# Banded attention by key blocks 0..127, 128..255, 256..271 instead of meta keys and window blocks

## The reference, cut to what matters

```python
k = k.reshape(b, L, A_KV_HEADS, A_HEAD_DIM)              # L = 272
s_loc = einsum(q_block, k_of_this_and_the_block_before) + bias   # masked outside the window of 128
s_meta = einsum(q_block, k[:, :16]) + bias
p = softmax(concat([s_meta, s_loc, sink]))
o = p[..., :16] @ v_meta + p[..., 16:272] @ v_local
x = LayerNorm(ALPHA * x + (o * silu(gate)) @ w_out)
```

## Time and profile before

| | |
|---|---|
| median of 3 runs | 956.26 us (954.53 to 956.31) |
| the profiled execution | 955.46 us |
| its span, first to last instruction | 953.2 us |
| TensorE busy | 918.1 us |
| VectorE busy | 553.1 us |
| ScalarE busy | 427.4 us |
| GpSimd busy | 65.1 us |
| mean granted clock of TensorE | 0.990 of full |
| bytes moved | 153.04 MB, mean 161 GB/s |

### The profile page before, as it was taken

How to read it: one execution, slowest core, us unless ns; L and a number is a source line. 1 busy time by engine, 2 the same in 40 slices (tenths; PEclk the granted TensorE clock), 3 DMA queues, 4 the chain that set the end, 5 groups by cost and what they waited for, 6 DMA issues and landing times.

```text
span 953.2 us, 18688 instructions
## 1 busy us (share of the span) xinstructions
PE 918.1 (96%) x7496; PEld 893.3 (94%) x7496; DVE 553.1 (58%) x713; ACT 427.4 (45%) x667; POOL 65.1 (7%) x86
## 2 busy tenths in 40 slices
PE   4999999999999999978999999999999999999995
PEld 4999999999899999978999999999999999999995
DVE  4457675676556666696645545453645546455556
ACT  5446556455455433344534344444444444443330
POOL 1220230233020000003000000000000000000000
PEclk9999999999999999989999999999999999999998
DMA  8745553554362354522544434534344444444522
GB/s 279 240 155 192 176 161 134 168 168 127 132 210 96 126 179 174 187 79 98 212 169 144 169 138 171 179 133 176 132 176 151 157 154 154 176 171 184 193 115 89
DMA packets 24530, 153.04 MB, mean 161 GB/s; under 512 B 3328, under 2 KB 3344, under 8 KB 7728
## 3 DMA queue, kind: packets, MB, share of 16 engines
q1 hardware_dynamic: 20736, 140.52, 40.5%
q0 software_dynamic: 2896, 7.70, 4.2%
q10 hardware_dynamic: 864, 4.33, 1.2%
HBM read 150.35 MB, written 2.18 MB: 160 GB/s over the span
## 4 chain that ended last, share of the span: by engine, by line
PE 88%; DVE 5%; DMA 3%; ACT 1%; issue 1%; SPq 0%; DVEq 0%; ACTq 0%
PE bank L246 73%; DMA raw<-chunks 3%; PE bank L334 2%; PE bank L521 2%; DVE w_lo L807 2%; PE bank L295 2%; ACT w_hi L545 1%; PE bank L315 1%; PE bank L400 1%; PE bank L436 1%; PE bank L414 1%; DVE h L1043 1%; PE bank L310 0%; PE bank L401 0%; PE bank L500 0%
## 5 line engine op out<-in xcount | busy, mean ns | idle before, releaser
L246 PE MATMUL bank<-x_hi,w_hi 128*128 128x272 f32 (+1 forms) x1536 | 445.9, 290 | 16.9 <-DVE w_lo L827 11.3
L246 PE MATMUL bank<-x_lo,w_hi 128*128 128x272 f32 (+1 forms) x1536 | 442.4, 288 | 0.0
L246 PE MATMUL bank<-x_hi,w_lo 128*128 128x272 f32 (+1 forms) x1536 | 442.1, 288 | 0.0
L807 DVE TENSOR_TENSOR w_lo<-raw,w_hi 128x2048 fp32r<-128x2048 f32 x130 | 303.2, 2339 | 217.2 <-ACT w_hi L545 217.2
L545 ACT ACTIVATE w_hi<-raw 128x2048 fp32r<-128x2048 f32 x130 | 248.3, 1912 | 214.4 <-PE bank L246 122.8
L246 PEld LDWEIGHTS bank<-x_hi,w_hi 128*128 128x128 f32 x1536 | 292.3, 190 | 19.7 <-DVE x_lo L813 11.0
L246 PEld LDWEIGHTS bank<-x_hi,w_lo 128*128 128x128 f32 x1536 | 291.8, 190 | 0.0
L246 PEld LDWEIGHTS bank<-x_lo,w_hi 128*128 128x128 f32 x1536 | 291.2, 190 | 0.0
L246 PE MATMUL bank<-og_hi,w_hi 128*128 128x272 f32 x256 | 74.9, 293 | 0.2 <-DVE og_lo L914 0.2
L246 PE MATMUL bank<-og_hi,w_lo 128*128 128x272 f32 x256 | 74.1, 289 | 0.0
L246 PE MATMUL bank<-og_lo,w_hi 128*128 128x272 f32 x256 | 73.7, 288 | 0.0
(11 more groups left out here) (190 smaller groups left out, 1009.7 us busy)
## 6 DMA issues: line engine op xcount, KB each, us to landing
raw<-chunks SPq DMA_DIRECT2D x130, 1024.0 KB, 4.8
work<-bias_table POOLq DMA_DIRECT2D x8, 512.0 KB, 5.6
work<-bias_table POOLq DMA_DIRECT2D x8, 256.0 KB, 6.8
work<-ln_rows ACTq DMA_DIRECT2D x1, 2048.0 KB, 8.0
out<-work SPq DMA_DIRECT2D x8, 256.0 KB, 2.4
h<-xT ACTq DMA_DIRECT2D x3, 544.0 KB, 12.4
raw<-chunks SPq DMA_DIRECT2D x4, 256.0 KB, 7.7
raw<-chunks SPq DMA_DIRECT2D x2, 512.0 KB, 14.3
```

The lines of the kernel that those rows point to most:

```text
L246: last = mm(o, l, r, start=(kt == 0 and n == 0), stop=(kt == KT - 1 and n == 2))
L807: V.tensor_tensor(w_lo[:, slot, :, :], raw[:, half, :, :], w_hi[:, slot, :, :].bitcast(f32), ALU.subtract).then_inc(lo_ready, 1)
```

## The change

The keys are cut at 0, 128 and 256 instead of at 0, 16 and 144. A head's turned probabilities lie in one bank and one buffer of 432 columns: `PT_M`, `PT_K1`, `PT_T`, `PT_K2` are its cuts. Columns 0..271 are keys 0..127 against the queries of all three blocks, 272..415 are keys 128..255 against the 144 queries that can see them, 416..431 are keys 256..271 against the last 16 queries. The turn has three transposes of 128 columns and three plain matmuls with the first 16 columns of the identity; these read all 128 partitions of a 16-column piece, and their outputs fill only partitions 0..15. So the rest of those columns of the bank, the 112 unused partitions of `a["t"][:, :, 416:432]` and those of `VL_cur` are cleared once. The value call has three steps, of 272, 144 and 16 columns, each over 128 partitions and each beginning at column 0 of `o_a`. ScalarE copies 128 x 432 for each head, and the copy of the meta part goes: `pt_copied` counts two for each pair of heads.

```diff
--- before.py
+++ after.py
@@ -36,6 +36,9 @@
 SW = 272 + 144 + 16
 
 
+PT_M, PT_K1, PT_T, PT_K2 = 256, 272, 400, 416
+
+
 B_K1, B_K2, B_Z = 256, 400, 416
 B_Q1, B_Q2 = BLK - META, SEQ - META
 
@@ -109,9 +112,9 @@
             assert at <= WORK, (at, WORK)
             return views
 
-        a = carve([("q", (2, T)), ("gate", (2, T)), ("og", (T,)), ("kT", (2, T)), ("V", (2, 256)), ("VM", (256,)),
-                   ("V_cur", (2, 128)), ("VM_cur", (128,)), ("bias", (4, SW)), ("t", (4, SW)),
-                   ("ptx", (2, 400)), ("pty", (512,)), ("neg_sink", (A_ITERS * 12,))])
+        a = carve([("q", (2, T)), ("gate", (2, T)), ("og", (T,)), ("kT", (2, T)), ("V", (2, 256)), ("VL", (256,)),
+                   ("V_cur", (2, 128)), ("VL_cur", (128,)), ("bias", (4, SW)), ("t", (4, SW)),
+                   ("pt", (2, SW)), ("neg_sink", (A_ITERS * 12,))])
         neg_sink = a["neg_sink"]
         setup = carve([("skip", (4000,)), ("onehot", (TAB,)), ("mask", (TAB,)), ("rel", (N_BUCKETS,)),
                        ("consts", (6, 128)), ("tab", (TAB,)), ("sink", (A_ITERS * 12,))])
@@ -124,7 +127,7 @@
         bank = [ctx.enter_context(nc.psum_tensor(f"bank{n}", [128, 512], f32)) for n in range(8)]
         acc = bank[0:2]
         scores = bank[2:4]
-        ptx_bank, pty_bank, o_a = bank[4:6], bank[6], bank[7]
+        pt_bank, tab_bank, o_a = bank[4:6], bank[6], bank[7]
         z_bank, o_b = bank[2:4], bank[5:7]
         last_acc = (bank[2:4], bank[4:6])
         k_acc_0 = bank[5:7]
@@ -164,7 +167,7 @@
 
 
 
-        PT_A, PV_A, O_A = 2 * 3 * A_ITERS, 4 * A_ITERS, 2 * A_ITERS
+        PT_A, PV_A, O_A = 2 * 2 * A_ITERS, 4 * A_ITERS, 2 * A_ITERS
 
         block = ctx.enter_context(nc.Block())
 
@@ -257,7 +260,7 @@
             project(P_K, x_hi, x_lo, ALL, x_from=(x_lo_ready, [lo for lo, _ in X_PARTS]), k_outer=True)
 
             pe.wait_ge(setup_loaded, 16 * 5)
-            mm(pty_bank[0:32, 0:LOC], setup["rel"][0:32, :], setup["onehot"][0:32, 0:LOC],
+            mm(tab_bank[0:32, 0:LOC], setup["rel"][0:32, :], setup["onehot"][0:32, 0:LOC],
                start=True, stop=True)
             mm(o_a[0:32, 0:T], setup["rel"][0:32, :], setup["onehot"][0:32, LOC:TAB],
                start=True, stop=True).then_inc(tab_psum, 1)
@@ -273,9 +276,9 @@
             def turn_value_a(u):
                 pe.wait_ge(tile_free[u], P_V + 1)
                 vT = a["gate"][:, u, :]
-                nc.tensor.transpose(ptx_bank[u][:, 0:128], vT[:, 16:144], ident[:])
-                nc.tensor.transpose(ptx_bank[u][:, 128:256], vT[:, 144:272], ident[:])
-                nc.tensor.transpose(ptx_bank[u][0:16, 256:384], vT[:, 0:16], ident[:]).then_inc(vt_ready, 1)
+                nc.tensor.transpose(pt_bank[u][:, 0:128], vT[:, 0:128], ident[:])
+                nc.tensor.transpose(pt_bank[u][:, 128:256], vT[:, 128:256], ident[:])
+                nc.tensor.transpose(pt_bank[u][0:16, 256:384], vT[:, 256:272], ident[:]).then_inc(vt_ready, 1)
             project(P_Q0, x_hi, x_lo, ALL, between=values_a)
 
             def scores_of(i, u):
@@ -303,16 +306,16 @@
                 n = 2 * i + pair
                 for b in range(2):
                     c = 2 * pair + b
-                    x, y, t = ptx_bank[b], pty_bank[0:16, 256 * b:256 * b + 256], a["t"][:, c, :]
+                    x, t = pt_bank[b], a["t"][:, c, :]
                     pe.wait_ge(probs_ready, 3 * (4 * i + c + 1))
                     if b == 0 and not (isinstance(n, int) and n == 0):
-                        pe.wait_ge(pt_copied, 3 * n)
-                    nc.tensor.transpose(y[:, 0:128], t[:, 0:16], ident[:])
-                    nc.tensor.transpose(y[:, 128:256], t[:, 272:288], ident[:])
-                    nc.tensor.transpose(x[:, 0:128], t[:, 16:144], ident[:])
-                    nc.tensor.transpose(x[:, 128:256], t[:, 288:416], ident[:])
-                    nc.tensor.transpose(x[0:16, 384:400], t[0:16, 416:432], ident[0:16, 0:16])
-                    nc.tensor.transpose(x[:, 256:384], t[:, 144:272], ident[:]).then_inc(pt_ready, 1)
+                        pe.wait_ge(pt_copied, 2 * n)
+                    nc.tensor.transpose(x[:, 0:128], t[:, 0:128], ident[:])
+                    nc.tensor.transpose(x[:, 128:PT_M], t[:, 272:400], ident[:])
+                    nc.tensor.transpose(x[:, PT_K1:PT_T], t[:, 128:256], ident[:])
+                    mm(x[0:16, PT_M:PT_K1], t[:, 416:432], ident[:, 0:16], start=True, stop=True)
+                    mm(x[0:16, PT_T:PT_K2], t[:, 400:416], ident[:, 0:16], start=True, stop=True)
+                    mm(x[0:16, PT_K2:SW], t[:, 256:272], ident[:, 0:16], start=True, stop=True).then_inc(pt_ready, 1)
 
             def value_a(i, pair):
 
@@ -321,18 +324,17 @@
                     pe.wait_ge(v_staged, 2 * (i + 1))
                 if not (isinstance(n, int) and n == 0):
                     pe.wait_ge(o_read, n)
-                pe.wait_ge(pt_copied, 3 * (n + 1))
-
-                for step in range(4):
+                pe.wait_ge(pt_copied, 2 * (n + 1))
+
+                for step in range(3):
                     for b in range(2):
                         cols = slice(64 * b, 64 * b + 64)
-                        x, y, o = a["ptx"][:, b, :], a["pty"][0:16, 256 * b:256 * b + 256], o_a[cols, 0:T]
-                        lo, n, l, r = ((0, 256, a["VM_cur"][0:16, cols], y),
-                                       (256, 16, a["VM_cur"][0:16, cols], x[0:16, 384:400]),
-                                       (0, 256, a["V_cur"][:, 0, cols], x[:, 0:256]),
-                                       (0, 128, a["V_cur"][:, 1, cols], x[:, 256:384]))[step]
-                        m = mm(o[:, lo:lo + n], l, r, start=(step == 0), stop=(step == 3))
-                        if step == 3:
+                        x, o = a["pt"][:, b, :], o_a[cols, 0:T]
+                        n, l, r = ((T, a["V_cur"][:, 0, cols], x[:, 0:PT_K1]),
+                                   (144, a["V_cur"][:, 1, cols], x[:, PT_K1:PT_K2]),
+                                   (16, a["VL_cur"][:, cols], x[:, PT_K2:SW]))[step]
+                        m = mm(o[:, 0:n], l, r, start=(step == 0), stop=(step == 2))
+                        if step == 2:
                             m.then_inc(pv_done, 1)
 
 
@@ -593,8 +595,8 @@
             for u in range(2):
                 act.wait_ge(vt_ready, u + 1)
                 A(a["V"][:, :, u * 128:(u + 1) * 128],
-                  ptx_bank[u][:, 0:256].rearrange("p (a b) -> p a b", b=128), ACT.Copy).then_inc(v_copied, 1)
-                A(a["VM"][0:16, u * 128:(u + 1) * 128], ptx_bank[u][0:16, 256:384], ACT.Copy).then_inc(v_copied, 1)
+                  pt_bank[u][:, 0:256].rearrange("p (a b) -> p a b", b=128), ACT.Copy).then_inc(v_copied, 1)
+                A(a["VL"][0:16, u * 128:(u + 1) * 128], pt_bank[u][0:16, 256:384], ACT.Copy).then_inc(v_copied, 1)
             split_hi(3, 1)
             def queries(P, i):
 
@@ -632,8 +634,7 @@
                     act.wait_ge(pv_done, 2 * n)
                 for b in range(2):
                     act.wait_ge(pt_ready, 2 * n + b + 1)
-                    A(a["ptx"][:, b, :], ptx_bank[b][:, 0:400], ACT.Copy).then_inc(pt_copied, 1)
-                A(a["pty"][0:16, :], pty_bank[0:16, :], ACT.Copy).then_inc(pt_copied, 1)
+                    A(a["pt"][:, b, :], pt_bank[b][:, 0:SW], ACT.Copy).then_inc(pt_copied, 1)
 
             def gate_tanh(P, i):
 
@@ -815,7 +816,8 @@
 
             V.memset(small[:], 0.0).then_inc(sink_ready, 1)
             for n in range(2):
-                V.memset(ptx_bank[n][:, 384:400], 0.0).then_inc(banks_cleared, 1)
+                V.memset(pt_bank[n][:, PT_M:SW], 0.0).then_inc(banks_cleared, 1)
+            V.memset(a["VL_cur"], 0.0).then_inc(banks_cleared, 1)
             def first_part_lo(n):
                 chunk, lo, hi = W_PARTS[n]
                 if hi == HALF:
@@ -840,7 +842,7 @@
                 split_lo(P, half)
             dve.wait_ge(setup_loaded, 16 * 5)
             dve.wait_ge(tab_psum, 1)
-            V.tensor_tensor(setup["tab"][0:32, 0:LOC], pty_bank[0:32, 0:LOC], setup["mask"][0:32, 0:LOC],
+            V.tensor_tensor(setup["tab"][0:32, 0:LOC], tab_bank[0:32, 0:LOC], setup["mask"][0:32, 0:LOC],
                             ALU.add).then_inc(tab_ready, 1)
             V.tensor_tensor(setup["tab"][0:32, LOC:TAB], o_a[0:32, 0:T], setup["mask"][0:32, LOC:TAB],
                             ALU.add).then_inc(tab_ready, 1)
@@ -914,6 +916,9 @@
                 V.tensor_tensor(og_lo[:, t, :], a["og"], og_hi[:, t, :].bitcast(f32),
                                 ALU.subtract).then_inc(og_lo_ready, 1)
 
+            dve.wait_ge(tab_stored, 16)
+            V.memset(a["t"][:, :, 416:SW], 0.0).then_inc(banks_cleared, 1)
+            dve.wait_ge(banks_cleared, 4)
             row_maxima(0)
             split_lo(4, 1)
             split_lo(5, 0)
@@ -1231,13 +1236,14 @@
```

(5 more changed lines are left out.)

## The result

The changed kernel took 946.24 us (median of 4 runs, 943.75 to 949.18) against 956.28 for the kernel before: ratio 0.9901, 95% interval 0.9878 to 0.9923. Timed twice more beside the kernel before, it came to 0.9867 (0.9849 to 0.9886) and 0.9901 (0.9884 to 0.9917). So it is 1.0 to 1.3% faster, 10 to 13 us; 940.5 us was forecast, with 936 to 947 as the range, and 15.7 us of gain.

A forecast was written before the change was run, and what follows sets the result against it. TensorE was taken to bound the kernel; value calls 8.6 us, nine turns 4.9 and seven turns between scores 2.2 sum to 15.7 us, bringing 956.26 to 940.5 us, range 936 to 947.

The forecast's parts named there:

- TensorE is the bound of this stage: Mixer A's loop over head groups: TensorE busy throughout a 32.69 us body, so its nanosecond is the kernel's.
- Value calls: Attention's value products: 1.64 us a call falls to 1.10, 0.54 less in each of 16, 8.6 us in all.
- padding to 128 rows costs nothing: Value call's last product: loading V's 16 rows padded with zeros to 128 was costed at nothing.
- Turns: Transposing probabilities: 0.52 us a head, 0.56 less a turn in nine (less 0.1 in all), 0.31 in seven between score calls.
- Between 128*16 and 128*128 it costs nothing: In the turn: stepping between loads of 16 and 128 columns, both over 128 rows, adds no switch cost.
- Sum: Whole kernel's gain: 8.6 us from value products, 4.9 from nine turns, 2.2 from seven between score calls, 15.7 us.
- forecast as summed: Whole kernel: 940.5 us, by itself 936 to 943.5, chance 0.76.
- draining rival: In the turn: small plain matmuls between full transposes drain the array, a head costs 0.75 us, kernel 946.1; chance 0.16.
- wait for L870: Between two score calls: TensorE newly waits 0.25 us for VectorE's read of the second score bank, in seven bodies.
- Weights' chain: Attention after scores: the chain from maxima to copies becomes the limit in seven bodies, gain only 8.0 us; chance 0.05.
- clock rivals: Attention: short passes and new waits bring half-clock stretches, 1.7 us lost each, kernel slower at 959; chance 0.03.
- copies in the second group: Second head group: TensorE arrives 0.56 us earlier, ScalarE's copies of turned probabilities 0.45, so 0.1 us is lost.

The follow-up runs named there:

- wide loads: Changed kernel with each head's three small turn matmuls loading 128 columns instead of 16 (output altered): 951.97 us, one run.
- columns back: Changed kernel with one more product of 224 columns per head in the value call, its result unread: 949.99 us.
- 16 rows: Changed kernel with the value call's last product reading 16 rows instead of 128 padded with zeros: 946.91 us, 0.9910 of the kernel before.
- squares: Changed kernel with each head's three small turn matmuls replaced by 16x16 transposes of rows 0..15: 942.52 us, 0.9858 of the kernel before.
- transposes: Changed kernel with the three small pieces as 128x16 transposes before the full ones (two pieces lost, output altered): 940.61 us, 0.9842 of the kernel before.
- grouped: Changed kernel with both heads' six full transposes first, then their six small matmuls: 941.26 us (0.9840 of the kernel before), again 942.81 (0.9869).
- grouped squares: Changed kernel with both heads' six full transposes first, then six 16x16 transposes for the small matmuls: 941.71 us, 0.9849 of the kernel before.
- small matmuls first: Changed kernel with both heads' six small turn matmuls before their six full transposes: 941.90 us, 0.9856 of the kernel before.

## Why the prediction came out as it did

- **TensorE is the bound of this stage: right.** It is busy in all of the changed kernel's body, and each edit's change (wide loads +1.01, columns back +0.76, 16 rows +0.30, squares -0.21, transposes -0.22, grouped -0.30, grouped squares -0.46 us a body) goes the way that TensorE's work changed. Where it shrinks between two score calls, VectorE's read takes part of it back.
- **Value calls, 16 x 0.54 = 8.6 us: right.** Measured 1.64 - 1.11 = 0.53, 8.5 us in all: 0.38 columns (shown by putting them back), 0.15 the passage (shown by putting it back). That padding to 128 rows costs nothing was argued from L310 and L312, which differ in columns loaded and not in rows; the measured call bears it out.
- **Turns: the step that failed.** "Between 128*16 and 128*128 it costs nothing" was read from 16-column transposes and carried over to plain matmuls, so a head was put at 0.52. It costs 0.72: 0.10 more going in, and 0.13 instead of 0.03 coming out. The same prediction charged a step of width at the ends of the value call, where it measured right (1.11 us against 1.10). A turn inside a projection gives 0.11 and not 0.56, one between score calls (213.56 to 215.10, 1.54 us, against 218.38 to 220.19, 1.81 us) 0.27 and not 0.31. 9 x 0.11 + 7 x 0.27 = 2.9 us instead of 7.1.
- **Sum.** 8.5 + 2.9 = 11.4 us, beside 7 x 1.45 = 10.2 in the seven bodies alone, 10.7 and 12.1 between runs of like mean clocks, 10.6 between profiles, and 10.0, 12.8 and 10.1 in the three timings. The spread of the clock is enough for these differences; that it makes all of them is not shown.
- **The range held because it took in the rival.** The forecast as summed, 936 to 943.5 with a chance of 0.76, missed with 946.24 (the later timings: 943.42 and 945.74). What lies inside 936 to 947 lies there because its upper end was drawn for the draining rival.
- **The wait for L870, now L872: right in place, absent in size.** VectorE's timeline, then TensorE's:

```profile
214.85 0.15 DVE L872 TENSOR_TENSOR work<-bank,work 16x16 f32<-16x16 f32 x1
```

```profile
215.10 0.39 PE L298 MATMUL bank<-og_hi,parts_r 64*128 64x272 f32 x2
```

  The read ends at 215.00, L298 starts at 215.10: with 0.06 for handing over, 0.04 is left before a wait begins. The longer turn filled the gap; the grouped versions, the squares and the small matmuls first opened it.
- **The draining rival** had it nearly whole: 0.75 a head, no wait on L870, 946.1. It got 0.16 because the rows of narrow transposes and of the scores were held to speak against it. The Trainium skill (TensorEngine Tiling, Key Properties) has a change of tiling mode drain TensorE. If a narrower load is such a change, the trace agrees for plain fp32 matmuls (0.10 us for 128*16, 0.09 for 128*64), and not for transposes of 16 columns or the scores of 64*16, which show no pause. The Trainium skill (TensorEngine Tiling, Restrictions) excludes transposes of fp32 input from column tiling, which would explain the former; no run shows the reason.
- **Weights' chain and clock rivals:** no wait on copies or weights in any body; the clock is 1.00 from 80 us to the end of the attention in all three profiles of the changed kernel. **The copies in the second group:** the wait of 0.3 us was to grow by 0.1, since TensorE would arrive 0.56 earlier; it is gone, since TensorE arrives only 0.11 earlier and the copies 0.45. In the second grouped profile, where the turn is shorter, the list has it again with 0.3 us.

## What to carry to other kernels

Count the changes of width and height between plain fp32 matmuls before counting columns: here each cost 0.10 us in and 0.13 to 0.18 out with the bare load, at 0.84 ns a column as much as 120 streamed columns or more. So pieces of one shape belong together, and padding a piece to its neighbours' rows cost less here than the change that it avoids (0.15 us). When pricing an operation by a neighbour in the trace, take one of the same kind as well as of the same shape. And before turning an engine that bounds faster, look how many hundredths of a microsecond the next engine's result is ahead: here it was 0.3 us between two score calls, and the grouped versions used it up. The fastest of the versions that compute the whole reference are the grouped ones, the squares and the one with the small matmuls first, 941 to 943 us, where the changed kernel took 943 to 946; their differences among themselves are within the intervals.

## What the runs showed of the hardware that was not expected

A plain fp32 matmul of 128*16 beside 128*128 work pauses TensorE 0.10 us, one of 128*64 behind a projection matmul 0.09; a transpose of 128*16 does not, and neither do score matmuls of 64*16 beside 64*128. A load of 128 fp32 columns that is covered only by 16 streamed columns takes 0.11 us, twice what the step from L315 to the next L310 had suggested. The same wait of 1.4 us is followed by a stretch at half clock in one execution (64.80 to 68.20) and by none in two others.
